# RWKV heads: level zero of a block inverse on VectorE (masked products, 32x32 transposes) in place of TensorE products with the identity

## The chip, the cores and the metric

One core of a Trainium2 chip runs the whole program. The metric is the time of one execution on the device in microseconds (us). Engines are named as the profile names them: PE (TensorE, the matmuls; PEld are its weight loads), DVE (VectorE), ACT (ScalarE), POOL (GpSimd) and SP (the queue that starts DMAs).

## What is computed

Two transformer blocks run one after the other on 256 tokens of width 1024. The first is a hybrid mixer (SSD and attention) with a hierarchical mixture of experts; the second is an RWKV-7 mixer beside a convolution, with a feed-forward layer behind. The change lies in the recurrence of the second block only. The reference writes it step by step:

```python
def frame_step(S, inp):
    r_t, w_t, k_t, v_t, kk_t, a_t = inp
    sa = jnp.einsum('bhvk,bhk->bhv', S, -kk_t)
    S = (S * w_t[:, :, None, :]
         + sa[..., None] * (kk_t * a_t)[:, :, None, :]
         + v_t[..., None] * k_t[:, :, None, :])
    o_t = jnp.einsum('bhvk,bhk->bhv', S, r_t)
    return S, o_t
```

There are 16 heads of size 64. Done in chunks of 128 tokens, this recurrence needs, for each head and chunk, the inverse of a unit triangular 128x128 matrix (identity minus the strict triangle of a gram matrix), which is then applied to the right-hand sides.

## The kernel before

Outside the heads the program streams weights from HBM, splits each block into a high and a low part (ACT line 311, POOL or DVE line 316) and multiplies them on PE (lines 322 to 340). The stage that the change touches, the heads, runs from about 911 us to about 1090 us of a span of 1334 us.

**Tiling.** Heads go in pairs, `PAIRS` = 8. A pair has four units `u = 2 * t + h` (two chunks `t` of 128 tokens, two heads `h`). `gram[c][:, u, :]` holds the four gram blocks of unit u, and buffers with index b or c alternate between pairs. Two groups g of two units (u = 2g + v) go through every step of the inverse.

**The inverse** has levels 0 to 6 (`LEV` = 7). At level `lev` diagonal blocks of 2^lev join into blocks twice as large. `Xs` (or `Xm`) holds the inverse so far, `XDs` (or `XD`) its transpose. A level is a chain over three engines: `below` on PE makes a product of the gram block with X into PSUM, `mask` on DVE copies it out times a constant mask into Y, `grow` on PE multiplies Y and XD to new blocks, `grown` on ACT copies these into X and XD. Blocks are 32x32 for levels under 5, in four row groups (`BLOCK`), then 64x64.

**Level 0 before.** DVE line 3163 (`begin_inverse`) turns the masked gram L into identity minus L, for two units at once, and counts `inverse_begun`. PE then has nothing to compute: for each unit and block it multiplies the gram block with the identity, once as the moving and once as the stationary operand (lines 2701 and 2704), only to bring the block and its transpose into PSUM. DVE line 3173 (`mask_first`) multiplies both with two 32x32 masks into X and XD and counts `y_masked`, for which `below` of level 1 (line 2709) waits.

**Order.** Each engine runs a program in the order in which it is written; there is no scheduler. `step(p, b)` runs the inverse of pair p. Between its levels stands work of two other pairs: the tail of pair p-1 (`rest`, `solve`, `state`, `outputs`; lines 2764, 2772, 2778 and 2779, 2791 to 2793) and the preparation of pair p+1 (`decays` line 2650, `turn_ar` 2658, `turn_bk` 2665, `grams` 2680). The gram masking of pair p+1 (DVE line 3153) and its `begin_inverse` stand on DVE behind the masks of levels 5 and 6 of pair p. In the first step (pair 0) parts of the convolution's projection stand in the gaps (`conv_part`, lines 322 to 324), in the last one nothing is prepared. PE's program is unrolled over all eight pairs; those of DVE and ACT loop over pairs 1 to 6, two in a round. `order.step` marks an instruction and waits for its end on the same engine, `order.mark` only marks it, `order.settle` waits for all that is marked.

The head of `step` on PE, with what stands between level 0 and level 1:

```python
if prep:
    decays(p + 1)
below(p, b, 0, (0,))
if tail:
    solve(p - 1, c, 0)
...
below(p, b, 0, (1,))
if tail:
    state(p - 1, c)
...
below(p, b, 1)
```

## Time and profile before

| | us |
|---|---|
| median of three runs | 1334.88 |
| lowest and highest | 1332.69, 1336.9 |
| the profiled execution | 1336.1 |
| its span in the trace | 1334.3 |

The profiled execution lies 1.2 us above the median, and its span 1.8 us below its own time. Over the span PE is busy for 1274.2 us (95%), DVE 819.0 (61%), ACT 733.9 (55%) and POOL 569.5 (43%). The mean clock granted to PE is 0.971 of full speed. The rows on which the prediction rests stand in their own section below. Times there are from the start of the span. In a timeline each row is a start, a length, an engine, a line, an operation with what it writes and reads, a count, and in brackets the idle time of the engine just before with what ended it; "issue" is idle time for which the profile shows no other engine as the cause. A matmul of float32 is shown as two (PE) with two weight loads (PEld).

### The profile page before, as it was taken

What the parts mean: (1) busy time and instruction counts of PE and PEld (TensorE: products, weight loads), DVE (VectorE), ACT (ScalarE), POOL (GpSimd) and SP (SyncE); (2) the same over time, 40 slices, a digit from 0 to 9 for tenths busy, and PEclk for the clock granted to TensorE, in tenths of its full rate; (3) what the DMA queues carried; (4) which work ended last, traced back from release to release, by engine and by line L of the source; (5) the groups of instructions that cost most, each with busy time, mean ns of one, the idle gap of its engine ahead of it and who ended that gap; (6) DMA issues with size and microseconds to landing.
All of it is one profiled execution on the core that took longest, in us unless ns stands there. A gap on an engine that the chain in (4) does not pass through costs nothing.

```text
span 1334.3 us, 26278 instructions
## 1 busy us (share of the span) xinstructions
PE 1274.2 (95%) x9849; PEld 1028.4 (77%) x9849; DVE 819.0 (61%) x1535; ACT 733.9 (55%) x1305; POOL 569.5 (43%) x252
## 2 busy tenths in 40 slices
PE   7999999998999999999899999899999999999997
PEld 6888878786787887878667877577777777788886
DVE  1576466537798988898467998855566653221213
ACT  5564566545676776666674233674344434554544
POOL 5886575250000000000479476555100017788884
PEclk9999999898899999999999999899799899999999
DMA  6654454157699989996476477433100006556662
GB/s 217 193 188 141 127 162 138 64 164 259 225 368 316 336 308 339 323 330 251 147 215 196 123 211 209 148 111 113 35 4 3 19 20 201 159 179 191 185 191 91
DMA packets 128529, 240.23 MB, mean 180 GB/s; under 512 B 16428, under 2 KB 23470, under 8 KB 128420
## 3 DMA queue, kind: packets, MB, share of 16 engines
q1 hardware_dynamic: 116656, 227.12, 52.0%
q10 hardware_dynamic: 11765, 11.59, 3.3%
q8 instruction: 77, 1.26, 0.4%
q14 instruction: 31, 0.25, 0.1%
HBM read 234.49 MB, written 1.05 MB: 177 GB/s over the span
## 4 chain that ended last, share of the span: by engine, by line
issue 44%; PE 29%; POOL 19%; DVE 4%; ACT 1%; DMA 1%; POOLq 0%; ACTq 0%; DVEq 0%
POOL wlo L316 19%; PE bank L340 4%; PE bank L336 4%; PE bank L337 4%; DVE bank L2440 2%; DMA work<-proj 1%; PE bank L2680 1%; PE bank L2731 1%; PE bank L2709 1%; PE bank L2792 1%; PE bank L2736 1%; PE bank L2772 1%; PE bank L2764 1%; PE bank L2793 1%; PE bank L2217 1%
## 5 line engine op out<-in xcount | busy, mean ns | idle before, releaser
L316 POOL TENSOR_TENSOR wlo<-raw,whi 128x1024 fp32r<-128x1024 f32 (+1 forms) x232 | 558.4, 2425 | 601.7 <-ACT whi L311 598.2
L311 ACT ACTIVATE whi<-raw 128x1024 fp32r<-128x1024 f32 (+1 forms) x300 | 311.9, 1054 | 256.6 <-PE bank L340 136.3
L336 PE MATMUL bank<-whi,t0h 128*128 128x512 f32 (+1 forms) x552 | 225.0, 408 | 6.6 <-ACT whi L311 4.9
L337 PE MATMUL bank<-whi,t0l 128*128 128x512 f32 (+1 forms) x552 | 218.9, 397 | 0.0
L340 PE MATMUL bank<-wlo,t0h 128*128 128x512 f32 (+1 forms) x552 | 151.5, 396 | 3.6 <-POOL wlo L316 3.6
L336 PEld LDWEIGHTS bank<-whi,t0h 128*128 128x128 f32 x552 | 105.5, 191 | 36.8 <-issue 7.6
L340 PEld LDWEIGHTS bank<-wlo,t0h 128*128 128x128 f32 x552 | 105.0, 191 | 28.8 <-POOL wlo L316 4.9
L337 PEld LDWEIGHTS bank<-whi,t0l 128*128 128x128 f32 x552 | 105.6, 191 | 23.2 <-issue 1.2
L316 DVE TENSOR_TENSOR wlo<-work,whi 128x1024 fp32r<-128x1024 f32 x96 | 113.0, 1219 | 7.6 <-ACT whi L311 7.6
L1670 PE MATMUL bank<-whi,t0h 128*128 128x512 f32 x256 | 106.6, 416 | 0.0
L1671 PE MATMUL bank<-whi,t0l 128*128 128x512 f32 x256 | 101.8, 398 | 0.0
L311 ACT ACTIVATE whi<-work 128x1024 fp32r<-128x1024 f32 x96 | 97.7, 1053 | 3.6 <-PE bank L1697 3.6
L2440 DVE SCALAR_TENSOR_TENSOR bank<-work,proj,bank 128x256 f32<-128x256 f32 x232 | 96.4, 484 | 1.6
L316 DVE TENSOR_TENSOR wlo<-raw,whi 128x1024 fp32r<-128x1024 f32 x68 | 81.7, 1240 | 12.4 <-ACT whi L311 12.1
L3609 DVE TENSOR_TENSOR bank<-bank,work 128x256 f32<-128x256 f32 x32 | 13.3, 427 | 112.8 <-ACT work L3534 112.8
L1675 PE MATMUL bank<-wlo,t0h 128*128 128x512 f32 x256 | 81.4, 399 | 0.0
L3080 POOL TENSOR_TENSOR proj<-proj,small x8 | 4.9, 617 | 145.7 <-PE bank L2793 145.7
L1675 PEld LDWEIGHTS bank<-wlo,t0h 128*128 128x128 f32 x256 | 48.1, 189 | 12.7 <-DVE wlo L316 1.1
L1670 PEld LDWEIGHTS bank<-whi,t0h 128*128 128x128 f32 x256 | 48.9, 191 | 11.0 <-issue 0.7
L1671 PEld LDWEIGHTS bank<-whi,t0l 128*128 128x128 f32 x256 | 48.7, 190 | 10.7 <-issue 0.7
L1693 PE MATMUL bank<-whi,t1h 128*128 128x512 f32 x128 | 50.8, 397 | 1.5 <-ACT whi L311 1.5
L1771 ACT ACTIVATE t1h<-bank 128x256 fp32r<-128x256 f32 x32 | 12.3, 384 | 70.4 <-PE bank L1681 70.4
(542 smaller groups left out, 2458.2 us busy)
## 6 DMA issues: line engine op xcount, KB each, us to landing
raw<-in_w_in SPq DMA_DIRECT2D x96, 512.0 KB, 3.6
raw<-in_w_ff SPq DMA_DIRECT2D x64, 512.0 KB, 4.2
work<-in_w_exp_down SPq DMA_DIRECT2D x68, 256.0 KB, 4.9
work<-in_w_exp_gate SPq DMA_DIRECT2D x62, 256.0 KB, 4.9
work<-in_w_exp_up SPq DMA_DIRECT2D x62, 256.0 KB, 5.7
raw<-in_w_exp_down SPq DMA_DIRECT2D x60, 256.0 KB, 4.7
raw<-in_w_in SPq DMA_DIRECT2D x20, 464.0 KB, 3.3
raw<-in_w_exp_gate SPq DMA_DIRECT2D x34, 256.0 KB, 5.2
```

What stands on the lines that cost most here:

```text
L311: nc.scalar.activation(whi[:, s, 0:width], raw_of(n)[:, 0:width], ACT.Copy).then_inc(hi_ready, 1)
L316: ins = (nc.vector if split_by_vector(n) else nc.gpsimd).tensor_tensor(wlo[:, s, 0:width], raw_of(n)[:, 0:width], whi[:, s, 0:width].bitca ...
L336: nc.tensor.matmul(dst[t][:, 0:width], hi[:, k, r], wh[:, kk, :], start=k == 0 and not begun, stop=False)
L337: nc.tensor.matmul(dst[t][:, 0:width], lo[:, k, r], wh[:, kk, :], start=False, stop=False)
L340: mm = nc.tensor.matmul(dst[t][:, 0:width], hi[:, k, r], wl[:, kk, :], start=False, stop=k == KC - 1)
L1670: nc.tensor.matmul(dst, t0h[:, k, r], wh[:, :, kk, :], start=k == 0, stop=False)
L1671: nc.tensor.matmul(dst, t0l[:, k, r], wh[:, :, kk, :], start=False, stop=False)
L1675: mm = nc.tensor.matmul(dst, t0h[:, k, r], wl[:, :, kk, :], start=False, stop=k == KC - 1)
L1693: nc.tensor.matmul(bank[4 + h][:, :], hh, whi[:, s, f], start=first, stop=False, skip_group_check=True)
L2217: nc.tensor.matmul(lora_middle(j), lora_in[:, k, c], hT[:, k, :], start=k == 0, stop=False)
L2440: ins = nc.vector.scalar_tensor_tensor(out=cvT[:, c, :] if w == W2 - 1 else partial(c), in0=uT[:, c, w:w + SEQ], scalar=tap, in1=partial(c ...
L2680: mm = nc.tensor.matmul(gram_bank(p, unit(h, t))[:, 256 * j:256 * j + 256], BK[r, j, t, :], ar, start=True, stop=True)
```

## The change

The kernel no longer makes level 0 on PE. `begin_inverse` on DVE, behind its identity-minus-gram instruction (now followed by a wait for its own end), writes X transposed itself: four products of a 32x32 gram block (two units at once, 32 partitions x 64 elements) with the mask, one for each row group, into `XDs` of the next pair. `turn_first` takes the place of `mask_first`: it waits for those products and for the last `grow` of the pair before, and makes X by two instructions that transpose 32x32 blocks on DVE. PE's `below` begins with level 1. The `state` product of pair p-1 moves from between levels 0 and 1 to behind `below` of level 1, and in the first step the two parts of the convolution stand together. Semaphore counts and the mask constants follow; `HEAD_DVE`, the number of marks in a round of DVE's loop, goes from 13 to 23.

```diff
--- before.py
+++ after.py
@@ -90,10 +90,7 @@
             continue
         block = np.tile((np.eye(64) + pick)[0:32, 0:32], (4, 1))
         if lev == 0:
-            turned = np.tile((np.eye(64) + pick.T)[0:32, 0:32], (4, 1))
-            put("level0_turned_first", turned)
-            put("level0", block)
-            put("level0_turned_last", turned)
+            put("level0_turned", np.tile((np.eye(64) + pick.T)[0:32, 0:32], (4, 1)))
         else:
             put(f"level{lev}", block)
     put("heads", (i[:, None] // 64 == i[None, :] // 64) * 1.0)
@@ -2590,7 +2587,6 @@
         SMALL = 5
         Xs, Ys = Ym[:, :, 0:32], Xm[:, :, 0:32]
         XDs = [XD[c][:, :, 0:32] for c in range(2)]
-        X_AND_XD = [carve(9216 + 256 * c, 2, 4, 64)[:, :, :, 0:32] for c in range(2)]
         Wn, Uo = carve(9984, NT, P), carve(10240, NT, P)
         SB = carve(10496, P)
         kk_row = carve(13296, D)
@@ -2601,8 +2597,7 @@
         kinv, hbonus, hvar = (tiny(24 + 32 * j, NT, NH) for j in range(3))
         hmean = tiny(120, 4)
         rk_loaded, kk_squared, kk_root = (sem(s) for s in ("rk_loaded", "kk_squared", "kk_root"))
-        cs_done, pdiff, inverse_begun = (
-            sem(s) for s in ("cs_done", "pdiff", "inverse_begun"))
+        cs_done, pdiff = sem("cs_done"), sem("pdiff")
         pexp = Again(exped, 4 * PAIRS)
         gram_masked = Again(mt_ready, 8)
         tok_ready = Again(rot_ready, NT * (IN_T - EVAC1))
@@ -2683,27 +2678,16 @@
                             mm.then_inc(gram_done.sem, 1)
 
 
-            def below(p, b, lev, pairs=(0, 1)):
-
-                for g in pairs:
-                    if lev == 0:
+            def below(p, b, lev):
+
+                for g in range(2):
+                    if lev == 1:
                         wait_from(pe, xt_copied, XT_COPIES * p)
-                        pe.wait_ge(inverse_begun, 2 * p + g + 1)
-                    elif lev == 1:
                         pe.wait_ge(*y_masked.at(2 * LEV * p + g + 1))
                     else:
                         pe.wait_ge(*xm_copied.at(2 * (LEV - 2) * p + 2 * lev + g - 3))
                     for v in range(2):
                         u = 2 * g + v
-                        if lev == 0:
-                            x, xd = (64, 0) if b == 0 else (0, 64)
-                            for r in BLOCK:
-                                nc.tensor.matmul(bank[g][r, x + v * 32:x + v * 32 + 32], gram[b][r, u, r], ident[r, r],
-                                                 start=True, stop=True)
-                            for r in BLOCK:
-                                mm = nc.tensor.matmul(bank[g][r, xd + v * 32:xd + v * 32 + 32], ident[r, r],
-                                                      gram[b][r, u, r], start=True, stop=True)
-                            continue
                         if lev < SMALL:
                             for r in BLOCK:
                                 mm = nc.tensor.matmul(bank[g][r, v * 32:v * 32 + 32], gram[b][r, u, r], Xs[r, u, :],
@@ -2807,18 +2791,14 @@
                     conv_part(5, 1)
                 if prep:
                     decays(p + 1)
-                below(p, b, 0, (0,))
                 if tail:
                     solve(p - 1, c, 0)
                 else:
                     conv_part(5, 2)
-                below(p, b, 0, (1,))
-                if tail:
-                    state(p - 1, c)
-                else:
                     conv_part(5, 3)
                 below(p, b, 1)
                 if tail:
+                    state(p - 1, c)
                     outputs(p - 1, c, 0, 0)
                 else:
                     conv_part(6, 0)
@@ -3090,7 +3070,7 @@
 
             return v.unsqueeze(3).to_broadcast([P, NT, heads, DH])
 
-        HEAD_DVE = 13
+        HEAD_DVE = 23
         GROUPS = ((0, 4), (4, 7), (7, 8))
 
         def dve_heads(dve, order):
@@ -3160,25 +3140,26 @@
                     g = slice(u - 1, u + 1)
                     dve.wait_ge(*gram_masked.at(4 * p + u + 1))
                     lt = gram[c][:, g, 0:P]
-                    nc.vector.scalar_tensor_tensor(out=lt, in0=lt, scalar=-1.0,
-                                                   in1=ident.unsqueeze(1).to_broadcast([P, 2, P]),
-                                                   op0=ALU.mult, op1=ALU.add).then_inc(inverse_begun, 1)
-
-            def mask_first(p, b):
-
-                at = CONST["level0_turned_first"][0] + 32 * b
-                pair = const[:, at:at + 64].rearrange("p (a s) -> p a s", a=2)
+                    order.step(nc.vector.scalar_tensor_tensor(out=lt, in0=lt, scalar=-1.0,
+                                                              in1=ident.unsqueeze(1).to_broadcast([P, 2, P]),
+                                                              op0=ALU.mult, op1=ALU.add))
+                    for r in BLOCK:
+                        order.mark(nc.vector.tensor_tensor(XDs[c][r, g, :], gram[c][r, g, r],
+                                                           con("level0_turned")[r].unsqueeze(1).to_broadcast([32, 2, 32]),
+                                                           ALU.mult))
+
+            def turn_first(p, b):
+
+                order.settle()
+                wait_from(dve, x_made, 2 * (LEV - 1) * p)
                 for g in range(2):
-                    dve.wait_ge(y_made, 2 * LEV * p + g + 1)
-                    nc.vector.tensor_tensor(X_AND_XD[b][:, :, 2 * g:2 * g + 2, :],
-                                            bank[g][:, 0:P].rearrange("p (a u s) -> p a u s", a=2, u=2),
-                                            pair.unsqueeze(2).to_broadcast([P, 2, 2, 32]), ALU.mult
-                                            ).then_inc(y_masked.sem, 1)
+                    nc.vector.transpose(out=Xs[:, 2 * g:2 * g + 2, :], in_=XDs[b][:, 2 * g:2 * g + 2, :]
+                                        ).then_inc(y_masked.sem, 1)
 
             def mask(p, lev):
 
                 for g in range(2):
-                    dve.wait_ge(y_made, 2 * LEV * p + 2 * lev + g + 1)
+                    dve.wait_ge(y_made, 2 * (LEV - 1) * p + 2 * lev + g - 1)
                     if lev < SMALL:
                         nc.vector.tensor_tensor(Ys[:, 2 * g:2 * g + 2, :],
                                                 bank[g][:, 0:64].rearrange("p (u s) -> p u s", u=2),
@@ -3217,7 +3198,7 @@
 
             def step(p, b, tail=True, prep=True):
                 c = 1 - b
-                mask_first(p, b)
+                turn_first(p, b)
                 if prep:
                     differences(p + 1)
                 else:
```

PE, the boundary between two pairs in the unrolled middle of the program, before (line 2650 is `decays`, 2701 and 2704 level 0, 2772 `solve`, 2778 and 2779 `state`, 2709 `below` of level 1, 2792 `outputs`):

```order
L2650 MATMUL bank<-proj,const 128x128 x2
L2701 MATMUL bank<-const,work 32x32 x4
L2704 MATMUL bank<-work,const 32x32 x4
L2701 MATMUL bank<-const,work 32x32 x4
L2704 MATMUL bank<-work,const 32x32 x4
L2772 MATMUL bank<-work 128x64 x2
L2701 MATMUL bank<-const,work 32x32 x4
L2704 MATMUL bank<-work,const 32x32 x4
...
L2778 MATMUL bank<-work 128x128
L2779 MATMUL bank<-proj,work 128x128
L2709 MATMUL bank<-work 32x32 x16
L2792 MATMUL bank<-work 128x64
```

The same place after (2645 is `decays`, 2756 `solve`, 2693 `below` of level 1, 2762 and 2763 `state`, 2776 and 2777 `outputs`, 2715 `grow`):

```order
L2645 MATMUL bank<-proj,const 128x128 x2
L2756 MATMUL bank<-work 128x64 x2
L2693 MATMUL bank<-work 32x32 x16
L2762 MATMUL bank<-work 128x128
L2763 MATMUL bank<-proj,work 128x128
L2776 MATMUL bank<-work 128x64
L2777 MATMUL bank<-proj,work 128x64
L2715 MATMUL bank<-work 32x32 x8
```

Sixteen matmuls of level 0 on each side of `solve` are gone, and `below` of level 1 now stands directly behind `solve`, ahead of `state`.

DVE, the same boundary before, from the masks of units 2 and 3 (line 3153) over `begin_inverse` (3163) to `mask_first` (3173) and the first work of `differences` (3107):

```order
L3153 TENSOR_TENSOR work<-bank,const 128x512
L3152 REGISTER_ALU
L3153 TENSOR_TENSOR work<-bank,const 128x512
L3161 REGISTER_ALU
L3163 SCALAR_TENSOR_TENSOR work<-work,const 128x2x128
L3172 ISA
L3173 TENSOR_TENSOR work<-bank,const 128x2x2x32
L3172 REGISTER_ALU
L3173 TENSOR_TENSOR work<-bank,const 128x2x2x32
L3107 ISA
```

And after, with 3133 for the masks, 3143 and 3147 for `begin_inverse`, 3156 for `turn_first`:

```order
L3133 TENSOR_TENSOR work<-bank,const 128x512
L3132 REGISTER_ALU
L3133 TENSOR_TENSOR work<-bank,const 128x512
L3141 REGISTER_ALU
L3143 SCALAR_TENSOR_TENSOR work<-work,const 128x2x128
L126 REGISTER_ALU
L3147 TENSOR_TENSOR work<-work,const 32x2x32 x4
L126 REGISTER_ALU
L157 REGISTER_ALU
L3156 STREAM_TRANSPOSE work<-work 128x2x32 x2
L3087 ISA
```

Between `begin_inverse` and level 1 stood a trip over PE and one instruction of DVE for each group; now six instructions stand in a row on DVE, behind a wait for line 3143, and there is no trip. The other `begin_inverse` (units 0 and 1) grows in the same way, ahead of the copies of level 6:

```order
L3141 REGISTER_ALU
L3143 SCALAR_TENSOR_TENSOR work<-work,const 128x2x128
L126 REGISTER_ALU
L3147 TENSOR_TENSOR work<-work,const 32x2x32 x4
L3162 REGISTER_ALU
L3171 COPY work<-bank 64x128
L3162 REGISTER_ALU
L3171 COPY work<-bank 64x128
```

It now has four products between 3143 and the copies of line 3171, which were line 3190.

## Rows read from the trace of the kernel before

**Rows 1.** The page, sections 1 and 3: busy time of PE; instruction fetches of PE.

```profile
PE 1274.2 (95%) x9849; PEld 1028.4 (77%) x9849; DVE 819.0 (61%) x1535; ACT 733.9 (55%) x1305; POOL 569.5 (43%) x252
...
q8 instruction: 77, 1.26, 0.4%
```

**Rows 2.** Windows: stretch; length; busy and count by engine; PEclk; DMA; GB/s.

```profile
935.26:962.63 27.37, 24.35 (x581) 20.67 (x581) 13.76 (x39) 8.56 (x38) 2.69 (x3) 0.69 0.15 42
982.59:1002.54 19.95, 18.41 (x582) 15.36 (x580) 13.22 (x39) 8.46 (x38) 1.34 (x2) 1.00 0.02 4
1022.31:1043.30 20.99, 19.51 (x581) 16.36 (x581) 13.24 (x39) 8.57 (x38) 1.34 (x2) 0.92 0.01 3
1043.30:1065.06 21.76, 20.06 (x573) 16.84 (x574) 12.62 (x38) 8.36 (x37) 1.34 (x2) 0.84 0.09 28
985.70:996.38 10.68, 9.86 (x421) 8.53 (x421) 7.15 (x24) 3.77 (x20) 1.34 (x2) 1.00 0.02 5
```

**Rows 3.** Timeline of PE, one pair boundary: start, us, work, [idle before].

```profile
1003.63 0.26 PE L2701 MATMUL bank<-const,work 32*32 32x32 f32 x8
...
1004.01 0.66 PE L2772 MATMUL bank<-work 128*128 128x64 f32 x4
1004.60 0.26 PE L2701 MATMUL bank<-const,work 32*32 32x32 f32 x8
...
1005.03 0.49 PE L2778 MATMUL bank<-work 128*128 128x128 f32 x2
...
1005.67 0.45 PE L2709 MATMUL bank<-work 32*32 32x32 f32 x32
1006.05 0.43 PE L2792 MATMUL bank<-work 128*128 128x64 f32 x2
...
1006.64 0.33 PE L2731 MATMUL bank<-work 32*32 32x32 f32 x16
```

**Rows 4.** Timeline of DVE, the same boundary.

```profile
1000.92 0.50 DVE L3190 COPY work<-bank 64x128 f32<-64x128 f32 x2
1002.04 1.29 DVE L3153 TENSOR_TENSOR work<-bank,const 128x512 f32<-128x512 f32 x2 [0.61 <-PE bank L2680]
1003.36 0.42 DVE L3163 SCALAR_TENSOR_TENSOR work<-work,const 128x256 f32<-128x256 f32 x1
...
1006.07 0.38 DVE L3183 TENSOR_TENSOR work<-bank,const 128x64 f32<-128x64 f32 x2 [0.25 <-PE bank L2709]
```

**Rows 5.** Timeline of DVE: an operation that waits for its own predecessor.

```profile
987.58 0.42 DVE L3118 TENSOR_TENSOR work<-work,small 128x256 f32<-128x256 f32 x1 [0.15 <-DVE work L3117]
```

**Rows 6.** Timeline of PE, heads stage: rows that PE began late for "issue".

```profile
942.87 0.26 PE L2731 MATMUL bank<-work 32*32 32x32 f32 x2 [3.00 <-issue]
...
976.05 0.29 PE L2731 MATMUL bank<-work 32*32 32x32 f32 x13 [1.04 <-issue]
...
989.86 0.28 PE L2731 MATMUL bank<-work 32*32 32x32 f32 x9 [0.17 <-issue]
...
993.37 0.25 PE L2736 MATMUL bank<-work 32*32 32x32 f32 x5 [0.65 <-issue]
...
1033.00 0.29 PE L2731 MATMUL bank<-work 32*32 32x32 f32 x12 [1.02 <-issue]
...
1052.42 0.63 PE L2772 MATMUL bank<-work 128*128 128x64 f32 x4 [1.36 <-issue]
```

**Rows 7.** DMA queues over the heads stage (905 to 1090 us).

```profile
q8 instruction: 37, 0.61, 1.4%
```

**Rows 8.** DMA in 991.0 to 992.1 us, 40 slices: one block of instructions.

```profile
GB/s 0 0 0 596 0 0 0 0 0 0 0 0 0 0 0 0 0 0 0 0 0 0 0 0 0 0 0 0 0 0 0 0 0 0 0 0 0 0 0 0
```

**Rows 9.** DMA in 934.0 to 937.2 us: nothing moves.

```profile
DMA packets 0, 0.00 MB, mean 0 GB/s; under 512 B 0, under 2 KB 0, under 8 KB 0
```

**Rows 10.** DMA in 937.0 to 940.6 us: weights of the second block.

```profile
q1 hardware_dynamic: 276, 0.80, 81.2%
```

**Rows 11.** Timeline of PE, last pair: the wait for ScalarE.

```profile
1068.29 0.49 PE L2778 MATMUL bank<-work 128*128 128x128 f32 x2 [0.57 <-ACT work L3003]
```

## The prediction, made before the changed kernel ran

> **What bounds the kernel now.** I read the page first: PE is busy for 1274.2 of 1334.3 us [rows 1], so time can leave only through PE's program or the gaps in it. Then I read the windows of single pairs. An undisturbed one, from `rest` to `rest`, takes 19.95 us, of which PE is busy for 18.41, and DVE for only 13.22 [rows 2]. Others take 27.37, 20.99 and 21.76 us at granted clocks of 0.69, 0.92 and 0.84 [rows 2]. So in the heads there are three prices: work in PE's queue, gaps, and stretches at the lower of PE's two clock levels (1.2 instead of 2.4 GHz).
>
> The timeline of PE at a pair boundary shows the first. Level 0 starts at 1003.63, `solve` at 1004.01, the second half of level 0 at 1004.60, `state` at 1005.03, `below` of level 1 at 1005.67, and no row has an idle time in brackets [rows 3]. Level 0 is nearly free of waiting: it costs what it occupies, 0.38 + 0.43 = 0.81 us of PE's queue for each pair. The mask on DVE that follows is hidden behind `solve` and `state`.
>
> The gaps are the second. The rows marked "issue" stand at places where PE has nothing to wait for: 3.00, 1.04, 0.65, 1.02 and 1.36 us [rows 6]. I looked at the DMAs at these moments. A queue of its own, q8, moves 77 pieces in the program, 1.26 MB [rows 1], so 16 KB each; PE's 9849 matmuls and 9849 weight loads divided by 77 are 256 instructions for a piece. One piece goes out at 991.1 us (in the fourth slice) [rows 8], and PE, which has stopped before, goes on at 993.37 [rows 6]; no other gap there has a cause. I read this as PE waiting for its own instructions. The heads take 37 of the 77 pieces in 14% of the time [rows 7], because 32x32 matmuls are short: 582 matmuls and as many loads in a pair [rows 2] are 4.5 pieces in 20 us.
>
> The Trainium skill (page "Runtime: NRT & Kernel Launch", section "Instruction fetch mechanics") describes blocks of 16 KiB, 256 instructions, fetched by a DMA queue of the sequencer. It says that a boundary is mostly hidden because instructions are dispatched more slowly than blocks arrive. The block size agrees with the counts [rows 1]; that it is hidden does not agree with the gaps [rows 6].
>
> **The change part by part.**
>
> *First step (pair 0).* PE is fed by the convolution there, which does not wait. Level 0 leaves the queue. I price it as at the later boundary [rows 3]: 0.81 us, less some 0.15 for DVE's longer chain, which lies behind two convolution parts: **-0.65** (bounds -0.8 and -0.4).
>
> *Six inner boundaries.* Here level 0 lies on both engines. PE without it would be ready for `below` of level 1 when `solve` ends. `solve` takes 1004.60 - 1004.01 = 0.59 us and would start at 1003.63, so that is 1004.22. But its input now comes from a chain on DVE, which starts where `begin_inverse` starts, at 1003.36, and ends that instruction at 1003.78 [rows 4]. The chain: a wait for its own end, 0.15 (the idle time before such an operation) [rows 5]; three products at a pace of 0.16 (0.38 for two of 0.22, line 3183, also 64 elements in each partition) [rows 4] and the last one in full, 0.22; a second wait, 0.15; the first transpose, 0.22. That is 1003.78 + 0.15 + 0.48 + 0.22 + 0.15 + 0.22 = 1005.00, and `below` begins 0.05 later, at 1005.05, after 0.83 us of idle PE. Behind it stand its own 0.38 (1005.67 to 1006.05), `state` with 0.64 (1005.03 to 1005.67) and `outputs` with 0.59 (1006.05 to 1006.64): `grow` of level 1 starts at 1006.66. It started at 1006.64 [rows 3]. The removed work is paid back as waiting: **0.0 for each boundary**. The trace has no transpose on DVE and no product on 32 partitions. From below I take waits of 0.03 (1003.33 to 1003.36, between the masks and line 3163) [rows 4] and a pace of 0.13, and get about 1004.65: -0.4 a boundary. From above I take the 0.42 us of a 256-element operation [rows 4] for the transpose and a pace of 0.21 (0.50 for two of 0.29, line 3190) [rows 4]: +0.4. So the term is 0, with bounds -2.4 and +2.4.
>
> The skill's page "VectorE: DVE Perf Modes", section "The three transpose paths", gives 311 ns for a 128x128 transpose in bf16. By that in place of my 0.22 the sum would be 0.5 us higher. Its section "Rules for kernel authors" says to minimize the number of operations, and the change puts twelve small ones where four stood. What that does is the slow rival below.
>
> *The other `begin_inverse`* (units 0 and 1) puts 0.15 + 4 x 0.16 = 0.8 us before the copies of level 6, which start at 1000.92 and end at 1001.42; the next masks wait idle for 0.61 us until 1002.04 [rows 4]. The copies would end at about 1002.2, just when `grow` of level 6 needs the second, and DVE hands on to the next row about 0.08 us before one ends (the pace of 0.21 against a length of 0.29, line 3190). So the masks would start within 0.1 us of 1002.04: cost 0, but the cover is used up, and what the products take beyond my price is lost in every pair.
>
> *Last step.* `state` waited 0.57 us for ACT, which loads a table [rows 11], and level 1 stood behind it. Now `below` goes first: **-0.3** (0 to -0.6).
>
> *Fewer instructions.* 64 of the 582 matmuls of a pair go, with their loads: 128 instructions, half a piece, leaving 4.05 pieces a pair. From level 1 to level 4 PE goes through 421 matmuls in 10.68 us [rows 2], 3.3 pieces, and a starved PE gets a piece in about 3.5 us (from the gap that ends at 989.86 to the one that ends at 993.37) [rows 6]. Level 0 put another 64 matmuls directly ahead of this; now PE idles there, which lets a piece arrive. Four of the gaps sum to 1.04 + 0.65 + 1.02 + 1.36 = 4.07 us [rows 6]. I expect a third less: **-1.3** (bounds -3 and +0.5, since the boundaries between pieces move).
>
> *The long gap.* PE stops from 939.87 to 942.87 [rows 6]. The piece that it lacks is asked for when the piece before begins, 256 instructions earlier, at about 936.5, and then meets weights: from 937 to 940.6 the weight queue takes 81% of the DMA engines and q8 moves nothing [rows 10]. With level 0 of pair 0 gone, the boundary between pieces lies half a piece later in the code: PE enters that piece near 933.3 (trace time of before), and asks in a stretch from 934.0 to 937.2 in which no DMA runs [rows 9]. The piece after that is asked for at the tail of the weights, where one got through before. I expect an ordinary gap of 0.7 in place of 3.00: **-2.3** (bounds -3 and 0).
>
> *The clock.* The pair with the long gap ran at 0.69 of the clock and took 27.37 us; one at 1.00 took 19.95 [rows 2]. Taking out the 3.00 gap, and the 0.65 of the other, the low clock cost 27.37 - 19.95 - 3.00 + 0.65 = 5.1 us. It fell when PE had stood still. The two others with a low clock also have gaps of over 1 us (1033.00 and 1052.42) [rows 6]; the gaps of 1.04 and 0.65 were not followed by one. Without the long gap I expect most of this back, but the new idle 0.8 us at each boundary can bring some of it elsewhere, for which I set 1.5 us, about the surplus of the pairs at 0.92 or 0.84 (20.99 and 21.76 against 19.95): **-3.6** (bounds -7.5, if all three stretches go, and +3).
>
> Sum: -0.65 + 0 - 0.3 - 1.3 - 2.3 - 3.6 = -8.15 us. From the profiled execution, 1336.1, that is 1327.95; the median lies 1.2 us lower, so 1326.8. I forecast **1327**.
>
> **The rivals.**
>
> *Fetches give nothing back.* The gaps only move: another piece meets the weights, or a gap of 3 us comes from something that stays. For it: the boundaries shift by half a piece each pair, and every second pair they fall where they fell before. Against it: the idle stretch and the busy one beside it [rows 9, 10]. Then -0.65 - 0.3 and about -1 of small gaps remain: 1333. By the page's rule that fetches are mostly hidden, only the first two terms would stand, 1334; the gaps are against it [rows 6], and I count it with this case.
>
> *All low stretches go.* With the clock term at its bound of -7.5 the sum is -12: 1323. Against it: two of these stretches follow gaps that the change only shortens.
>
> *DVE becomes the bound.* Products and transposes at the upper prices make `below` of level 1 late by 0.4 us at each boundary, and the same products delay the copies of level 6 and with them the next masks by 0.4. Seven times 0.8 is 5.6 us. PE then idles for over 1.2 us in one piece at each boundary, as long as the gaps after which the clock fell; one us a pair (20.99 against 19.95) is 6 more. Less the fetch and end terms of -4.5, that is +7: 1342. It decides from `below` of level 1 starting later than 1.6 us before 1006.64, thus 1005.03 on the scale of [rows 3]; my estimate stands on that point.
>
> *The change doesn't do what it says.* The order lists show level 0 gone from PE and no new work there, so I give this no chance.
>
> **How the numbers follow.** About 0.3%, 4 us, is what a measurement of this kernel can tell from no change. Forecast 0.46, all stretches gone 0.16, fetches give nothing 0.26, DVE bound 0.12. Faster by over 4 us are the first two, 0.62; within 4 us the third, 0.26; slower the fourth, 0.12. The range reaches from 1320 to 1336: it leaves out the slow case and the far end of the second, some 0.18, and holds the bounds of the inner boundaries.
>
> **What would show it.** Lines 2701 and 2704 are gone, and PE has 8 x 64 = 512 fewer matmuls and q8 four fewer pieces. At the boundaries PE idles 0.5 to 1.1 us before `below` of level 1, released by DVE's transposes; a transpose takes 0.2 to 0.3 us, a product about 0.2. `grow` of level 1 comes within 0.4 us of where it came, counted from `rest`. The gap near 940 us is under 1.5 us and the pair with 0.69 of the clock is gone, its time near 20 to 22 us. Wrong would be: a gap of 3 us still there; more pairs under 0.95 of the clock than three; masks of line 3153 that no longer wait for PE.

## The result, and the profile after

The changed kernel takes 1355.57 us (median of 4 runs, 1348.63 to 1358.85), the kernel before on the same chip 1335.86 us (4 runs, 1332.69 to 1336.9). The ratio is 1.0145, 95% interval 1.0099 to 1.0191. I had forecast 1327, with 1336 as the upper end of the range. The change makes the kernel slower by 1.5%. In two of the later kernels and in one set of runs of the kernel before, one execution each counts as slow; ratios, intervals and means leave these three out, medians don't.

The profiled run of after is its fastest, 1348.63 us (span 1346.8, before 1334.3). Its page, sections 1 and 3 (compare [rows 1]):

```profile
PE 1277.1 (95%) x9337; PEld 1033.1 (77%) x9337; DVE 840.2 (62%) x1599; ACT 734.3 (55%) x1305; POOL 570.2 (42%) x252
...
q8 instruction: 73, 1.20, 0.4%
```

512 matmuls are gone, and four blocks of instructions with them, as the prediction said. Yet PE is busy for 2.9 us *more*. That happens only where the same work runs more slowly. The windows of the eight pairs, `rest` to `rest` (the first from `below` of level 1), show it (columns as in [rows 2], PEclk is the third from the right):

```profile
914.42:938.03 23.61, 20.48 (x496) 14.84 (x496) 15.22 (x36) 9.14 (x33) 7.07 (x3) 0.86 0.16 51
938.03:962.90 24.87, 24.53 (x514) 21.43 (x514) 14.49 (x47) 8.34 (x36) 1.34 (x2) 0.60 0.13 42
962.90:983.80 20.90, 18.01 (x523) 15.01 (x521) 15.20 (x47) 8.58 (x38) 1.35 (x2) 1.00 0.01 4
983.80:1005.15 21.35, 18.69 (x518) 15.64 (x517) 14.78 (x47) 8.48 (x38) 1.34 (x2) 0.92 0.01 3
1005.15:1025.40 20.25, 17.61 (x519) 14.84 (x517) 14.86 (x47) 8.46 (x38) 1.34 (x2) 1.00 0.01 3
1025.40:1049.50 24.10, 22.41 (x518) 19.17 (x517) 14.96 (x47) 8.54 (x38) 1.34 (x2) 0.72 0.01 3
1049.50:1073.60 24.10, 22.32 (x517) 19.19 (x517) 14.93 (x47) 8.51 (x38) 1.34 (x2) 0.72 0.07 24
1073.60:1098.00 24.40, 21.90 (x500) 17.90 (x500) 12.20 (x34) 8.63 (x38) 1.34 (x2) 0.72 0.01 3
```

At a granted clock of 1.00 a pair takes 20.25 to 20.90 us, 0.3 to 0.95 more than the 19.95 of before [rows 2], though it holds 64 matmuls fewer. And three pairs near the end, which the kernel before ran at 0.84 or higher, stand at 0.72 and take 24.1 to 24.4 us. Six of the eight pairs are under 0.95 of the clock (before: three), one of the signs of being wrong that I had named.

The same boundary that stood ahead of the prediction, on PE (compare [rows 3]; `rest` is now line 2748, `solve` 2756, `below` 2693, `state` 2762, `grow` 2715):

```profile
1004.54 0.68 PE L2736 MATMUL bank<-work 64*64 64x64 f32 x8 [0.26 <-DVE work L3171]
1005.15 0.66 PE L2748 MATMUL bank<-proj,work 128*128 128x64 f32 x4
...
1006.26 0.63 PE L2756 MATMUL bank<-work 128*128 128x64 f32 x4
1007.99 0.50 PE L2693 MATMUL bank<-work 32*32 32x32 f32 x32 [1.09 <-DVE work L3156]
1008.41 0.49 PE L2762 MATMUL bank<-work 128*128 128x128 f32 x2
...
1009.45 0.33 PE L2715 MATMUL bank<-work 32*32 32x32 f32 x16
```

and on DVE (compare [rows 4]; 3133 are the masks, 3147 the products, 3156 the transposes, 3171 the copies of level 6):

```profile
1001.42 1.29 DVE L3133 TENSOR_TENSOR work<-bank,const 128x512 f32<-128x512 f32 x2 [0.27 <-PE bank L2675]
1002.74 0.42 DVE L3143 SCALAR_TENSOR_TENSOR work<-work,const 128x256 f32<-128x256 f32 x1
1003.20 0.96 DVE L3147 TENSOR_TENSOR work<-work,const 32x64 f32<-32x64 f32 x4
1004.19 0.50 DVE L3171 COPY work<-bank 64x128 f32<-64x128 f32 x2
1004.72 1.29 DVE L3133 TENSOR_TENSOR work<-bank,const 128x512 f32<-128x512 f32 x2
1006.05 0.42 DVE L3143 SCALAR_TENSOR_TENSOR work<-work,const 128x256 f32<-128x256 f32 x1
1006.50 0.96 DVE L3147 TENSOR_TENSOR work<-work,const 32x64 f32<-32x64 f32 x4
1007.60 0.37 DVE L3156 STREAM_TRANSPOSE work<-work 128x64 f32<-128x64 f32 x2
```

Between 1001.42 and the transposes DVE has no idle time in brackets any more: the masks at 1004.72 no longer wait for PE, as those of before did for 0.61 us (a second of the signs named; over the heads these masks waited 13 times before and 6 times now). PE waits for this row of work twice, 0.26 us before `grow` of level 6 and 1.09 us before `below` of level 1.

PE's waits in the heads, summed by what ended them (line waited at, releaser, us in total, times, longest). Before, from the first `below` of level 1 to the last `grow` of level 6:

```profile
PE bank L2731 <- issue: 5.5, 5, 3.0
PE bank L2680 <- ACT work L2966: 2.0, 5, 0.4
PE bank L2772 <- issue: 1.4, 1, 1.4
...
PE bank L2736 <- issue: 1.0, 2, 0.6
PE bank L2709 <- issue: 0.9, 2, 0.5
```

After, the same stretch:

```profile
PE bank L2693 <- DVE work L3156: 9.5, 7, 3.0
PE bank L2736 <- DVE work L3171: 4.0, 7, 2.4
PE bank L2675 <- ACT work L2946: 2.4, 6, 0.4
...
PE bank L2720 <- issue: 1.2, 2, 0.9
PE bank L2715 <- issue: 0.7, 1, 0.7
PE bank L2693 <- issue: 0.5, 1, 0.5
...
PE bank L2702 <- issue: 0.2, 1, 0.2
```

The waits for instructions fell from 5.5 + 1.4 + 1.0 + 0.9 = 8.8 us to 1.2 + 0.7 + 0.5 + 0.2 = 2.6 us, and the gap of 3.00 [rows 6] is gone. Waits for DVE, of which before had none, came with 13.5 us. Two of them are about as long as the old gap, 2.97 and 2.40 us, and have one cause. Timelines of DVE, then POOL, then PE in the first pair:

```profile
909.56 2.58 DVE L3147 TENSOR_TENSOR work<-work,const 32x64 f32<-32x64 f32 x2
```

```profile
909.44 2.38 POOL L313 TENSOR_TENSOR wlo<-raw,whi 128x1024 fp32r<-128x1024 f32 x1 [0.39 <-ACT whi L308]
```

```profile
914.42 0.65 PE L2693 MATMUL bank<-work 32*32 32x32 f32 x32 [2.97 <-DVE work L3156]
```

and in the second:

```profile
933.79 3.10 DVE L3147 TENSOR_TENSOR work<-work,const 32x64 f32<-32x64 f32 x4
```

```profile
934.46 2.34 POOL L313 TENSOR_TENSOR wlo<-raw,whi 128x1024 fp32r<-128x1024 f32 x1 [5.39 <-ACT whi L308]
```

```profile
937.27 0.83 PE L2736 MATMUL bank<-work 64*64 64x64 f32 x8 [2.40 <-DVE work L3171]
```

Two of the 64 products last 2.36 and 2.34 us in place of 0.22: each was issued just behind an operation of POOL and ended with it.

**The clock in all runs.** A run's time at the lower level is 2 x (1 - mean granted clock) x its time, since the lower level (1.2 GHz) is half the upper (2.4). Over 110 runs of the kernel before this has a mean of 73.7 us, at a mean time of 1336.2; over the four of after, 125.3 us at 1354.7. Inside one kernel, from run to run, each such microsecond costs 0.37 us (before) and 0.34 (after); pooled over all kernels of this study it is 0.35. So 51.6 us more at the lower level are worth 18.1 of the 18.4 us between the means. **By this measure the change is worth about nothing at equal clock; the loss is the clock.** Below, "at equal clock" is a mean time less that of before, less 0.35 for each microsecond more at the lower level. It is a correlation; the runs with filled gaps test it. Such figures don't tell differences under some 2 us apart: the kernel before itself varies by 1.2 us in them from chip to chip.

### The profile page after: what moved, and what is told of

Same layout as the page of the kernel before. It is cut to its first block and busy times, and to the rows that moved or that the text cites. A ratio compares the mean times of both kernels' runs of the same rounds, so it can differ in the third digit from the quotient of the medians.

```text
span 1346.8 us, 25330 instructions
## 1 busy us (share of the span) xinstructions
PE 1277.1 (95%) x9337; PEld 1033.1 (77%) x9337; DVE 840.2 (62%) x1599; ACT 734.3 (55%) x1305; POOL 570.2 (42%) x252
## 5 line engine op out<-in xcount | busy, mean ns | idle before, releaser
L3590 DVE TENSOR_TENSOR bank<-bank,work 128x256 f32<-128x256 f32 x32 | 13.3, 428 | 112.4 <-ACT work L3515 112.4
L1672 PEld LDWEIGHTS bank<-wlo,t0h 128*128 128x128 f32 x256 | 48.2, 189 | 12.7 <-DVE wlo L313 1.2
```

Of the source, the lines that this page charges most:

```text
L1672: mm = nc.tensor.matmul(dst, t0h[:, k, r], wl[:, :, kk, :], start=False, stop=k == KC - 1)
L3590: nc.vector.tensor_tensor(bank[b][:, SEQ:2 * SEQ], bank[b][:, 0:SEQ], ff_part[:, b, :], ALU.add).then_inc(ff_summed.sem, 1)
```

## The experiments

My theory (**clock theory**): PE's new idle time behind DVE lets the clock fall, and the slow clock is most of the loss. Rivals: DVE's longer row costs it all by its own waiting; the held products do; the place of `below` does. Each ratio below is to the kernel before on the same chip.

**The order of `state` and `below`** (against after):

```
-                below(p, b, 1)
                 if tail:
                     state(p - 1, c)
+                below(p, b, 1)
```

> The changed kernel with state of pair p-1 put back in front of below of level 1, where it stood in the kernel before. In the changed kernel PE idles about 1.1 us before below of level 1 (released by DVE's transpose) in each pair and does state (0.64 us) behind it. Theory A (PE waits for a longer chain on DVE, and its clock falls because of the idle time): state fills half of the idle time, below starts where it started, and everything behind comes 0.6 us earlier in each of seven pairs: about 4 us; if the clock falls less often, up to 15 us, so 1335 to 1351 against about 1355. Rival B (the time is lost to PE's instruction fetches, which moved): no more than the 4 us. Rival C (the order of state doesn't matter, DVE sets the end of each pair): below 2 us.

Measured: 1351.97 us, ratio 1.0108 (1.0054 to 1.0162). `below` then waits for no transpose in a steady pair, but `state` waits for ScalarE's copy: 3.1 us in seven waits. Part of the wait changed its name: PE's waits in the heads sum to 19.2 us, after 20.5, and the heads run at 0.80. The place of `below` isn't what made the loss; whether it is worth the 3.6 us between the medians, four runs of each can't tell.

**Filled gap**: four products of constants before `below` of level 1 (against after).

```
+                if tail:
+                    for _ in range(4):
+                        nc.tensor.matmul(bank[0][:, 384:512], con("centred"), con("ones"), start=True, stop=True)
                 below(p, b, 1)
```

> The changed kernel with four matmuls of constants (128x128 by 128x128, about 0.3 us each, into a free part of PSUM bank 0, read by nobody) between solve and below of level 1 in pairs 1 to 7, where PE idles for about 1.1 us. They take no part in the result. Theory A (the clock falls because PE stands idle there): the pairs at a granted clock of 0.72 (24.1 us) go back to 1.00 (about 20.5), which is 3 pairs x 3.6 = 11 us of 19: about 1344. The matmuls cost up to 0.1 us a pair where they outlast the wait. Rival B (the clock falls for another reason, such as the fetches or the first two long waits alone): same time or 1 us more, and the clock of these pairs stays near 0.72.

Measured: 1342.86 us, ratio 1.0042 (1.001 to 1.0073), for work that is of no use. PE's timeline at the boundary:

```profile
1006.22 1.11 PE L2801 MATMUL bank<-const 128*128 128x128 f32 x8
1007.48 0.63 PE L2693 MATMUL bank<-work 32*32 32x32 f32 x32
```

The heads as one window each (first `below` of level 1 to last `grow` of level 6), of before, of after, and of this kernel:

```profile
916.85:1083.92 167.07, 153.76 (x4532) 126.78 (x4532) 103.93 (x287) 68.18 (x290) 16.49 (x17) 0.92 0.06 19
```

```profile
914.43:1096.87 182.44, 164.80 (x4083) 137.08 (x4084) 116.63 (x345) 67.94 (x290) 16.47 (x17) 0.81 0.06 17
```

```profile
917.89:1085.33 167.44, 150.03 (x4139) 124.33 (x4140) 116.42 (x345) 67.92 (x290) 16.47 (x17) 0.96 0.06 19
```

56 matmul records more, and PE is busy for 14.8 us less, at a granted clock of 0.96 in place of 0.81. Each window is of one execution, for after and for this kernel the fastest; over all executions the time at the lower level has a mean of 70.9 us in place of 125.3. PE had more to do and the kernel got 12 us faster by the means, so the slow clock is what most of the loss consists of. The fillers aren't free: at equal clock this kernel lies 7.0 us above before, as PE's waits hardly fall (19.7 us after 20.5). The gap was also what let instruction blocks arrive: waits for "issue" are 7.1 us again, after 2.6.

What in the idle time lets the clock fall isn't shown by this. The trace with `state` first has nearly the same waits (19.2 us, 7.0 of them for DVE, here 19.7 and 7.4), but ran at 0.80 in place of 0.96. So the clock follows neither sum. The fillers also put 128x128 products where PE had no work, and whether it is this work or the closed gap that counts wasn't tried apart.

**All products in one group of partitions.** Leaves out the level-0 multiplication by the gram (the inverse starts from constants). There are as many operations, with as many elements in each partition; the first of the four now covers 128 partitions.

```
-                    for r in BLOCK:
-                        order.mark(nc.vector.tensor_tensor(XDs[c][r, g, :], gram[c][r, g, r], ...
+                    order.mark(nc.vector.tensor_tensor(XDs[c][:, g, :], turned, turned, ALU.mult))
+                    for r in BLOCK[1:]:
+                        order.mark(nc.vector.tensor_tensor(centred_sq[BLOCK[0], :, r], gram[c][BLOCK[0], g, r], ...
```

> The changed kernel with the four products of begin_inverse all starting on partition 0 instead of on 0, 32, 64 and 96: the first writes the mask itself on 128 partitions, the other three multiply on partitions 0 to 31 into a spare place. It leaves out the multiplication of the masks with the gram in level 0, so the result is not the reference's; the number and size of the operations stay. In the changed kernel a product of 0.216 us starts 0.247 us after the one before, without overlap. Theory A1 (operations that start in another group of 32 partitions than the one before wait for its end, as the VectorE page of the Trainium skill says): the pace falls to 0.16 us, the chain is shorter by 4 x 0.09 = 0.35 us for each begin_inverse, PE's idle time before below falls from 1.1 to below 0.6 us, 4 us in all and more if the clock recovers. Rival A2 (small products with both inputs in SBUF have that pace anyway): pace 0.25, time as the changed kernel.

Measured: 1342.82 us, ratio 1.0021 (0.9993 to 1.005). DVE's timeline:

```profile
1002.92 0.22 DVE L3147 TENSOR_TENSOR work<-const 128x64 f32<-128x64 f32 x1
1003.06 0.47 DVE L3149 TENSOR_TENSOR work<-work,const 32x64 f32<-32x64 f32 x3
```

Four operations take 0.61 us in place of 0.96: their pace is 0.13 to 0.14 in place of 0.25. So a product costs what it does because it starts in another group of 32 partitions than the one before. PE waits for DVE for 7.8 us in place of 13.5, and at the boundary for 0.74 us in place of 1.09 (I had expected less than 0.6). The Trainium skill (page "VectorE: DVE Perf Modes", section "Two Vector instructions with no wait between them") says that an instruction that starts in another quadrant than the last one read or wrote begins only when all earlier ones have finished. This trace agrees: 0.25 of pace against 0.22 of length is one after the other.

**The kernel before with eight extra products a pair** (results unused), behind a wait for `begin_inverse`'s own end, which the cut doesn't show:

```
+                    for r in BLOCK:
+                        order.mark(nc.vector.tensor_tensor(centred_sq[r, :, 0:32], gram[c][r, g, r], ...
```

> The kernel before, level 0 on PE as it was, with the eight products a pair of the changed kernel added on DVE behind begin_inverse (same shapes and places, written to a spare buffer that nobody reads). Nothing is left out. Theory A (the price of the change lies on DVE in front of level 6's copies and of level 0's masks): level 0's mask comes later by about 1.1 us a pair, so 7 x (0.5 to 1.4) = 4 to 10 us slower than before, with clock loss up to 20 us. Rival B (the price lies in PE's shorter program and moved fetches): within 2 us of before, 1335.

Measured: 1345.9 us, ratio 1.0055 (1.0018 to 1.0091): a good third of the loss by the ratios (9.4 of 18.4 us by the means; the interval allows from an eighth to over a half) comes from DVE's operations alone, with level 0 still on PE. `grow` of level 6 waits for DVE as in after:

```profile
1005.54 0.68 PE L2752 MATMUL bank<-work 64*64 64x64 f32 x8 [0.34 <-DVE work L3196]
```

**Short operations on POOL** (against after). Six low parts are cut to 8 columns, so most of the low halves of these weight tiles are left out.

```
-                split_low(pool, n)
+                split_low(pool, n, width=QF if n < Q_CONV + 6 else 8)
```

> The changed kernel with the low part of six weight blocks on POOL (the last two of the convolution, the first four of the output projection behind the heads) cut from 1024 to 8 columns; it leaves out the rest of these low parts, so the result is not the reference's. In the changed kernel the first product of begin_inverse lasts 2.34 us instead of 0.216 two times (pairs 0 and 1), each time beginning within 0.15 us of a POOL subtraction of 2.4 us, and PE waits 2.97 and 2.40 us behind it. Theory P (DVE operations with both inputs in SBUF wait for a POOL operation that reads SBUF): no product over 0.3 us is left, both waits of PE fall below 1.2 us, about 4 us come back, and the clock of the first two pairs with it (up to 5 us more): 1341 to 1351. Rival (the products are slow for a reason of DVE's own, such as its instruction fetch): the 2.3 us products stay.

Measured: 1346.84 us, ratio 1.0114 (1.0048 to 1.0179). No product lasts long, and PE's wait in the first pair is 0.85 us in place of 2.97:

```profile
917.40 0.46 PE L2693 MATMUL bank<-work 32*32 32x32 f32 x32 [0.85 <-DVE work L3156]
```

So POOL is what held them. The Trainium skill (page "SBUF — State Buffer", section "SBUF: two separate sides") says that a VectorE operation with two SBUF inputs and a GpSimd operation share a pair of ports, which the first takes for its whole instruction. This case agrees: 2.36 us for a product of 0.22. The waits of 1.1 before `below` stay in each pair. By the ratio (1.0114 after 1.0145) most of the loss stays too, though the two intervals overlap.

**Copies of level 6 on ScalarE**, with `state` first (against after): `mask(p, 6)` goes from DVE, and after `diagonal` ScalarE does

```
+                    nc.scalar.copy(Ym[HALF[1], 2 * g:2 * g + 2, :],
+                                   bank[g][HALF[1], 0:P].rearrange("p (u s) -> p u s", u=2)).then_inc(y_masked.sem, 1)
```

> The changed kernel with state in front of below of level 1 (as in e1_state_first) and the two copies of level 6 on ACT instead of DVE. These copies stand on DVE behind the first begin_inverse and delay the masks of units 2 and 3. Theory A (DVE's row of work between the grams and below is what PE waits for): DVE's row is 0.53 us shorter, PE's wait before grow of level 6 (0.26 us) goes, below starts 0.5 us earlier; 7 x 0.5 = 3.5 us less than e1_state_first, 1345 to 1350. ACT has room for two copies of 0.26 us. If the clock stays high more often, down to 1338.

Measured: 1342.76 us, ratio 1.0062 (1.0028 to 1.0096). In steady pairs PE waits for DVE no more, but for ScalarE (0.35 us), and the interval overlaps with that of `state` first alone, so the shorter row isn't priced by it. One block of instructions came late as in before:

```profile
1064.09 0.22 PE L2715 MATMUL bank<-work 32*32 32x32 f32 x3 [2.87 <-issue]
```

**The kernel before with its instruction blocks shifted**: 32 tiny matmuls (128 instructions, half a block) in the convolution of the first step.

```
+                    for _ in range(32):
+                        nc.tensor.matmul(bank[0][0:32, 384:416], con("centred")[0:32, 0:32], con("ones")[0:32, 0:32],
+                                         start=True, stop=True)
```

> The kernel before with 32 matmuls of constants (32x32, about 9 ns each in the queue) in the first step of the heads, written to a free part of PSUM bank 0 and read by nobody: 128 instructions, half a piece of PE's instruction stream, about 0.4 us of PE. It tests the term of the prediction on the long gap: the 3.00 us gap near 940 us comes from a fetch that meets the weights. If that is so, the gap goes to below 1.5 us as every fetch boundary behind it moves by half a piece, and the low clock after it may go too: 1328 to 1335 against 1335 to 1338 of the kernel before. If the gap has another cause it stays at 3 us.

Measured: 1333.68 us, ratio 0.9993 (0.9966 to 1.002). The gap of 3.00 us [rows 6] shrank, though not below the 1.5 us that I had expected, and the heads ran at 0.96 in place of 0.92:

```profile
946.75 0.29 PE L2731 MATMUL bank<-work 32*32 32x32 f32 x12 [1.86 <-issue]
```

So where a block ends bears on that gap; over ten runs it is worth no time that can be measured, and by the interval at most 4.5 us. My terms for the gap and its clock, -5.9 us together, are more than that.

**Three fillers, copies on ScalarE** (the edits of the filled gap and of the copies together, `below` first):

> The changed kernel with three matmuls of constants before below of level 1 (0.3 us each, as in e2_fill, not part of the result) and the copies of level 6 on ACT. Theory A: the clock stays high as in e2_fill and the row of work on DVE is 0.5 us shorter a pair: 3 us less than e2_fill, 1338 to 1342, thus about the kernel before. If the chain on DVE were not the cause: as e2_fill.

Measured: 1339.91 us, ratio 1.0032 (1.0001 to 1.0063). This can't be told from the filled gap alone (1.0042): once the gap is filled, a shorter row on DVE brings nothing that the ratios show. At equal clock this kernel lies lower (1.9 us above before, in place of 7.0), with one filler less and on another chip, so that a few us may be in the two changes together. The wait of 3.0 us in the first pair is still there.

**Both cures: four fillers and short operations on POOL**, and the same with three fillers and copies on ScalarE:

> The changed kernel with both cures at once: the four constant products ahead of below of level 1 in the steps of pairs 1 to 7, and the eight low parts on POOL that fall beside VectorE's products of the first step cut to 8 columns (so it leaves out most of the low halves of these eight weight tiles). If the loss is the clock in the heads plus the two held products, as the runs with either cure say, it comes to -3 to +1 us of the kernel before (1332 to 1336) with less than 28 us of low clock in the heads and no PE wait over 2 us near 914 or 937. If a third loss is there, the longer inverse itself (rest to grow of level 1 4.30 us in place of 4.10), it stays 2 to 6 us above the kernel before.

> As the run before it, with three constant products in place of four and the two copies of level 6 on ScalarE in place of VectorE. If VectorE's row of work ahead of the transposes is the last part of the loss, this one is below the kernel before by 2 to 6 us (1329 to 1333); if the wait was covered by the constant products anyway, it stands at the time of the run before it within 2 us.

Measured: 1329.25 us, ratio 0.9954 (0.9921 to 0.9987; one of its ten executions, of 6358 us, stands apart), and 1332.24 us, ratio 0.9973 (0.9936 to 1.0011). With the two cures nothing of the loss is left, and the first lies 6 us below the kernel before (by the interval 2 to 11), where 3 was my best case. Moving the copies adds nothing to them. The traces show six short operations on POOL, not the eight of the expectation. Part of POOL's work is missing here, so this is no version to use, and as the kernel before wasn't run with the same cut, its part in the gain is open.

**Control: fillers in the kernel before.**

```
                         pe.wait_ge(*y_masked.at(2 * LEV * p + g + 1))
+                        if fill and g == 0:
+                            for _ in range(4):
+                                nc.tensor.matmul(bank[0][:, 384:512], con("centred"), con("ones"), start=True, stop=True)
```

> Control: the kernel before with the same four constant products, put behind the wait of below of level 1 (bank 0 isn't free ahead of it there). If the products win only by holding the clock up where it falls, and it falls in the kernel before for 27 us of the heads only, they pay their own 0.4 to 0.9 us in seven pairs and give back at most 4 us: -1 to +5 us. If they are a gain to any kernel of this form, it comes to -6 to -2 us and the comparison of the filled changed kernel with the unfilled kernel before was not fair to the latter.

Measured: 1340.78 us, ratio 1.004 (1.0008 to 1.0072). Where no gap is there to fill, they cost their own time. They took 7 us off the mean time at the lower level here, 54 us in the changed kernel. So they raise the clock mainly where there is a gap, though there is also less low clock to win back here.

**The complete version: four fillers, and four of POOL's tiles in four pieces each.** The cut shows the loop for one tile:

```
+                for x in range(0, QF, 256):
+                    ins = nc.gpsimd.tensor_tensor(wlo[:, s, x:x + 256], raw_of(n)[:, x:x + 256],
+                                                  whi[:, s, x:x + 256].bitcast(F32), ALU.subtract)
+                ins.then_inc(lo_by_pool, 1)
```

> A version that leaves nothing out: the changed kernel with the four constant products, and the low parts on POOL that fall beside VectorE's first products worked off in four pieces of 256 columns each (same work, POOL waits 3 us and more between these tiles). If a product of VectorE is held only until POOL's running instruction ends, it waits at most about 0.6 us in place of 2.4, and the run comes near the one with cut low parts: -8 to -1 us of the kernel before. If POOL's next piece gets in ahead of the waiting product, it is held for the whole tile again and the time is that of the filled kernel, +3 to +8 us of the kernel before.

Measured: 1335.96 us, ratio 0.9996 (0.9974 to 1.0018): nothing computed is left out, and the loss is gone, but nothing is gained. That lies between the two outcomes expected, near the first. The longest product now lasts 0.74 us, but each of four can be held (DVE, then POOL, then PE in the first pair):

```profile
912.55 2.76 DVE L3158 TENSOR_TENSOR work<-work,const 32x64 f32<-32x64 f32 x4
```

```profile
912.43 2.79 POOL L669 TENSOR_TENSOR wlo<-raw,whi 128x256 fp32r<-128x256 f32 x4 [0.38 <-ACT whi L308]
```

```profile
917.10 0.45 PE L2701 MATMUL bank<-work 32*32 32x32 f32 x32 [2.65 <-DVE work L3167]
```

In the first pair the four products still take 2.76 us, and PE waits 2.65 in place of 2.97. In the second pair the pieces helped: the four take 1.48 us in place of 3.10, and PE waits 0.78 us in place of 2.40.

**Control: the pieces in the kernel before**, and **two fillers in place of four** with the pieces:

> Control: the kernel before with the low parts on POOL beside the first step in four pieces of 256 columns. It has one operation of VectorE that a whole tile holds (line 3125, 2.48 us, near 920 us), and PE shows no wait for it. If the hold costs only where the change put products into a row on which PE waits, this stands within 2 us of the kernel before. If shorter holds help any kernel of this form, it comes to -8 to -3 us, and the comparison of the piecewise changed kernel with the kernel before was not fair.

> The changed kernel with the same pieces on POOL and two constant products a pair in place of four. If the four cost their own time on the path (7 pairs x 4 x 0.24 us, as the unfilled control suggested), two cost 3 us less, and the clock stays as with four: -6 to -2 us of the kernel before. If it is the busy time of PE that holds the clock up, two are too few: low clock comes back for part of the heads, and the time is +2 to +10 us.

Measured: 1334.38 us, ratio 0.9981 (0.9942 to 1.002), which can't be told from the kernel before; that the hold costs nothing where PE doesn't wait for the held row fits it, but a few us would not show. And 1340.59 us, ratio 1.0014 (0.9967 to 1.0062), no better than with four (0.9996): two fillers leave PE a wait of 0.60 us in steady pairs, and the heads run at 0.94 in place of 0.98. The interval holds both outcomes expected in part. The low clock that came back (a mean of 70.0 us in place of 58.1) speaks for the second: fewer are not shown to be cheaper.

## Why the prediction was wrong, step by step

- **The clock, -3.6: this step failed, by its sign.** I had written that the pair with the long gap would recover, and put 1.5 us for what "the new idle 0.8 us at each boundary" might cost. The recovery came nowhere (0.60 at 938 to 962 us), and three more pairs went to 0.72. In the heads the window grew from 167.07 to 182.44 us: idle time by 4.3 (13.3 to 17.6), PE's busy time by 11.0, although level 0 left seven of its pairs (7 x 0.81 = 5.7 us). So 16.7 us of it is slower running. For all of this I had set 1.5 us, about the surplus of one pair at 0.92 or 0.84, and +3 as the worst sum of the term. It is the term whose error is the size of the loss. Why the clock falls in one pair and not in the next with the same 1.1 us wait (20.25 us at 1.00 beside 24.10 at 0.72) stays open, and so does what it follows. Among the kernels without fillers the time at the lower level roughly grows with PE's waits for DVE in the heads: 74 us with none, 90 and 91 with 4.3 and 4.5 us of waits, 116 with 7.0, 98 with 7.8, 114 with 10.3 and 125 with 13.5. With four fillers it is 71 us at 7.4.
- **Six inner boundaries, 0.0: mis-sized, and the point of balance was crossed.** From `rest` to `grow` of level 1 it is 4.30 us (1005.15 to 1009.45), before 4.10 (1002.54 to 1006.64), where I had 4.12. From the start of line 3143 to `below` I had 1.69 us and measured 1.94. The products took 0.96 in place of 0.70: their pace was 0.25, not 0.16, which I read from a row of operations that all start at partition 0. The two waits were 0.03 and 0.13 us, not 0.15; the first transpose 0.245, not 0.22; and PE began 0.15 behind it, not 0.05. Counted from `rest`, `below` came at 2.84 us, where its turning point (1005.03) was 2.49; the work behind it took 1.46 us in place of my 1.61, so `grow` is only 0.20 late. (My bounds of 0.4 a boundary were rounded up: their terms give -0.33 and +0.35.)
- **The other `begin_inverse`, cost 0: failed.** "The cover is used up" was right, and with 0.96 in place of 0.8 us it was overdrawn: 0.26 us before `grow` of level 6 in each pair. With the 0.20 above, six boundaries cost 2.8 us, of which I had 0. The inner boundaries alone (1.2) stayed within their bounds.
- **First step, -0.65: failed.** PE waits 2.97 us there for the transposes. I covered DVE's chain by the convolution and didn't look at POOL, whose operations of 2.4 us run beside the heads' start. A sign was in the trace of before: there line 3125 takes 2.48 us just behind an operation of POOL.
- **Last step, -0.3: the wait went, the time didn't.** `state` waits no more where it had waited for 0.57 us [rows 11]. But two waits stand ahead of it that level 0 had filled, one for ScalarE before `solve` and one for DVE before `below`:

```profile
1073.53 0.66 PE L2748 MATMUL bank<-proj,work 128*128 128x64 f32 x4
1074.64 0.63 PE L2756 MATMUL bank<-work 128*128 128x64 f32 x4 [0.46 <-ACT work L2979]
1076.33 0.67 PE L2693 MATMUL bank<-work 32*32 32x32 f32 x32 [1.06 <-DVE work L3156]
```

From `rest` to `below` it is 2.80 us, as in the inner pairs (2.84), and with their 1.46 from there to `grow` the sum is 4.26 us, before 4.31: -0.05 in place of -0.3. In fact it was 4.73 us, as the clock fell behind `below` (0.82 from 1076.33 to 1078.26).
- **Fewer instructions and the long gap, -1.3 and -2.3: held, and by more.** Waits for "issue" fell by 6.2 us against my 3.6. For the long gap the trace agrees with the reason given: one block arrives between 934.0 and 937.3 us, ahead of the weights, and none between 937.3 and 941.0, while the weights take 78% of the DMA engines. But PE also stood for 2.40 us at 937.27 waiting for DVE, so the run doesn't tell the two apart. The waits that went are also the other side of the same coin: with the idle time filled they are 7.1 us again. A wait for a block that runs during a wait for DVE isn't a gain beside it.

The sum at equal clock, from the waits: +13.5 (DVE) - 6.2 (issue) + 0.5 (ScalarE, 4.4 after 3.9) - 6.5 (level 0, 8 x 0.81) = +1.3 us; the runs say +0.4. So -8.15 had two errors: 5.0 us in the terms that aren't the clock (-4.55 against +0.4), and 21.7 in the clock term (-3.6 against +18.1). The outcome was the third rival's, "DVE becomes the bound": `below` came later than its turning point, and the waits and the clock did what it says. Its price for the waiting was too large (5.6 us, measured 2.8), its price for the clock too small (6 us, measured 18.1): 1342 became 1355.6.

What isn't settled beside that: the kernel with both cures has a mean 6.6 us below the one with POOL's work in pieces, and its waits for DVE are only 2.5 us less (3.1 and 5.6). Part of it may be POOL's missing work; that wasn't tried apart.

## What to carry to other kernels

Moving work off a saturated engine pays only if the engine doesn't then stand waiting for it: here 6.5 us of PE's work turned into 13.5 us of PE's waiting, and the kernel lost by the clock, not by the exchange itself. Price the new wait first at the granted clock of the trace and then at the lower one, and give the second case a real chance wherever the trace shows both levels. For many small operations on VectorE, read the pace from a row whose operations start at *different* partitions, and look at what POOL runs beside them.

## What the runs showed of the hardware

- A VectorE product of 32x64 in fp32 lasts 0.22 us. Four in a row take 0.96 us when each starts in another group of 32 partitions, and 0.61 when all start at partition 0 (the first of them then on 128 partitions).
- A product with both inputs in SBUF that is issued behind a POOL operation ends with it: 2.36 in place of 0.22 us. With POOL's work in pieces of 0.7 us several products in a row are held: four take 2.76 us at one place and 1.48 at another, in place of 0.96.
- A transpose of 128x64 in fp32 in blocks of 32x32 on VectorE takes 0.20 to 0.25 us.
- Constant products with no use made the kernel 12.7 us faster (1355.57 to 1342.86), with a granted clock in the heads of 0.96 in place of 0.81. At equal clock the 28 matmuls of 128x128 cost about 7 us in both kernels.
- Nearly equal waits of PE (19.2 and 19.7 us in the heads) went with granted clocks of 0.80 and 0.96.
- PE's waits for its own instructions were 8.8 us before, 2.6 beside 13.5 us of waits for DVE, and 7.1 again when the gap was filled: what blocks cost shows only where PE doesn't wait for something else.
